# Zero products first, low parts by tile, outputs by column halves: another order at the two ends and the choice of a two-layer trunk

## The reference

```
x = x + concat(window_sink_attention(...), gated_retention(...)) @ w_out[l]    # from rms_norm(x) @ w_in[l], 2304 columns
h = rms_norm(x, ln_ffn[l])
y = swiglu(h, ...) if l == 0 else moe_swiglu(h, ...)       # D_FF = 2816
x = x + y
...
def moe_swiglu(h, router_w, w_gate, w_up, w_down):
    top_val, top_idx = lax.top_k(h @ router_w, 2)          # 2 of 8 experts for each token
    gates = sum over the two of one_hot(top_idx) * softmax(top_val)
    return sum over e of gates[..., e] * swiglu(h, w_gate[e], w_up[e], w_down[e])
...
return rms_norm(x, ln_final)
```

## Time and profile before

| | |
|---|---|
| median of 3 runs | 1190.61 us (1189.17 to 1190.63) |
| profiled execution: time, span | 1190.02 us, 1188.0 us |
| TensorE matmul, weight load busy | 1167.3 us (98%), 981.9 us (83%) |
| VectorE, ScalarE, GpSimd busy | 975.7 us (82%), 828.6 us (70%), 30.9 us (3%) |
| HBM read | 342.06 MB, 289 GB/s over the span |
| weight load to landing, experts | 7.0 us for 1 MB (median) |

### The profile page before, as it was taken

One profiled execution on the slowest core, in us unless ns is written; L12 is line 12 of the kernel. 1 busy time (PEld: TensorE's weight loads), 2 busy tenths in 40 slices (PEclk: granted clock), 3 DMA queues, 4 the chain that ended last, 5 costly groups with the idle time before them and its releaser, 6 DMA issues.

```text
span 1188.0 us, 18370 instructions
## 1 busy us (share of the span) xinstructions
PE 1167.3 (98%) x6010; PEld 981.9 (83%) x6010; DVE 975.7 (82%) x1101; ACT 828.6 (70%) x1007; POOL 30.9 (3%) x43
## 2 busy tenths in 40 slices
PE   7999999999999999999999999999999999999996
PEld 7997888888998788888888888888888888888885
DVE  4867555545675999999899999989999989999996
ACT  6655554534653788878778778868887877887884
POOL 0400000000120000000000000000000000000000
PEclk9999999999999999999999999999999999999999
DMA  9955655556444399999899999989999999999960
GB/s 284 370 182 164 196 192 194 177 183 207 142 161 142 109 376 364 395 342 368 330 338 369 372 373 360 355 331 347 362 396 342 361 336 338 375 365 368 366 238 35
DMA packets 142614, 344.64 MB, mean 290 GB/s; under 512 B 6112, under 2 KB 64688, under 8 KB 142528
## 3 DMA queue, kind: packets, MB, share of 16 engines
q1 hardware_dynamic: 141952, 342.34, 80.3%
q0 software_dynamic: 352, 1.09, 0.4%
q10 hardware_dynamic: 224, 0.10, 0.1%
HBM read 342.06 MB, written 1.44 MB: 289 GB/s over the span
## 4 chain that ended last, share of the span: by engine, by line
PE 91%; DVE 4%; ACT 2%; DMA 2%; issue 1%; SPq 0%; DVEq 0%; ACTq 0%
PE psum L1144 87%; PE psum L1141 4%; DMA raw<-in_w_in 1%; DVE prob L900 1%; DVE w_lo L381 0%; DVE smax L884 0%; DVE score L880 0%; ACT w_hi L372 0%; DMA skew<-bias_rows 0%; DVE nmax L885 0%; ACT aT_hi L590 0%; DVE x_sb L828 0%; ACT squares L578 0%; ACT aT_hi L726 0%; ACT w_hi L392 0%
## 5 line engine op out<-in xcount | busy, mean ns | idle before, releaser
L399 DVE TENSOR_TENSOR w_lo<-raw,w_hi 128x1024 fp32r<-128x1024 f32 x528 | 627.3, 1220 | 40.9 <-PE psum L1144 15.7
L392 ACT ACTIVATE w_hi<-raw 128x1024 fp32r<-128x1024 f32 x528 | 550.2, 1061 | 110.1 <-PE psum L1144 108.3
L1144 PE MATMUL psum<-w_hi,aT_hi 128*128 128x512 f32 (+1 forms) x1232 | 447.2, 372 | 1.4 <-ACT w_hi L372 0.6
L1144 PE MATMUL psum<-w_hi,aT_lo 128*128 128x512 f32 (+1 forms) x1232 | 440.0, 366 | 0.0
L1144 PE MATMUL psum<-w_lo,aT_hi 128*128 128x512 f32 (+1 forms) x1232 | 323.3, 366 | 0.8 <-DVE w_lo L381 0.7
L1144 PEld LDWEIGHTS psum<-w_hi,aT_hi 128*128 128x128 f32 x1232 | 233.4, 189 | 38.6 <-issue 1.8
L1144 PEld LDWEIGHTS psum<-w_hi,aT_lo 128*128 128x128 f32 x1232 | 233.6, 190 | 35.0
L1144 PEld LDWEIGHTS psum<-w_lo,aT_hi 128*128 128x128 f32 x1232 | 214.6, 189 | 40.4 <-DVE w_lo L399 1.8
L381 DVE TENSOR_TENSOR w_lo<-raw,w_hi 128x1024 fp32r<-128x1024 f32 x118 | 144.8, 1234 | 48.7 <-PE psum L1144 44.6
L372 ACT ACTIVATE w_hi<-raw 128x1024 fp32r<-128x1024 f32 x118 | 124.6, 1059 | 82.4 <-PE psum L1144 74.2
L1144 PE MATMUL psum<-w_hi,heT_hi 128*128 128x512 f32 x352 | 138.1, 392 | 0.0
(11 more groups left out here) (179 smaller groups left out, 638.5 us busy)
## 6 DMA issues: line engine op xcount, KB each, us to landing
raw<-in_exp_w_down SPq DMA_DIRECT2D x88, 1024.0 KB, 7.1
raw<-in_exp_w_gate SPq DMA_DIRECT2D x80, 1024.0 KB, 7.0
raw<-in_exp_w_up SPq DMA_DIRECT2D x80, 1024.0 KB, 6.9
raw<-in_w_in SPq DMA_DIRECT2D x17, 1024.0 KB, 5.4
raw<-in_ffn_w_gate SPq DMA_DIRECT2D x22, 512.0 KB, 4.0
raw<-in_ffn_w_up SPq DMA_DIRECT2D x22, 512.0 KB, 5.1
raw<-in_ffn_w_down SPq DMA_DIRECT2D x11, 1024.0 KB, 5.0
raw<-in_w_out SPq DMA_DIRECT2D x8, 1024.0 KB, 8.1
```

Source lines behind the costliest of these rows:

```text
L392: nc.scalar.activation(w_hi[:, q % HIGHS, :], raw_piece(slot, q % 2), ACT.Copy).then_inc(hi_made, 1)
L399: eng.tensor_tensor(w_lo[:, q % LOWS, :], raw_piece(e_slot[q // 2], q % 2), w_hi[:, q % HIGHS, :].bitcast(F32), ALU.subtract).then_inc(lo_ ...
L1144: return pe.matmul(dst, a, b, start=start, stop=stop, skip_group_check=True)
```

## The change

- **Start, TensorE.** VectorE clears two tiles of `aT_lo` first of all (its copy of the table rows moves behind the low part of piece 1). TensorE multiplies 8 products of zeros before it waits for anything loaded. The gain rows are turned before x. x's first half is turned, 6 more products of zeros follow, then piece 0, and only then x's second half. The bias products move from behind piece 0 to behind piece 1 and to other banks, and TensorE's wait for their copy moves from piece 2 to the turn of q and k.
- **Start, loads.** The first weight half is issued between the two halves of x; the second gain load moves from SP's queue to ScalarE's, ahead of the other one there.
- **Start, ScalarE.** The high part of piece 0 comes after two tiles of x, not four.
- **Choice.** `keep_busy` does 10 and 5 products instead of 8 and 3 behind the logits and the ranks. The gather goes by part and token tile, with a wait for one tile's low part at a time. ScalarE makes the high parts of pieces 0, 1 and 2 ahead of the loop (one of them ahead of the exponential) and has its table load there as well. VectorE splits the first two gathered banks and makes the low part of piece 0 ahead of the experts' weights and of the loop.
- **Experts.** Spreads and additions go by column halves: (half, tile) instead of (tile, half).
- **End.** The last two pieces go by column halves, so that the first half is announced (`down_half`) after six of the twelve products. ScalarE squares four half rows instead of two whole ones; one factor chain for both token tiles instead of two.

The diff, cut to its core:

```diff
-WARM_COPY, WARM_CHOICE, WARM_MARK = 2, 8, 3
+EARLY = 3
+WARM_COPY, WARM_CHOICE, WARM_MARK = 2, 10, 5
+START_BUSY, FIRST_BUSY = 8, 6
...
             load_x(0)
-            sp.dma_start(gain_rows[0:2 * DK, :], ln_mix.rearrange("l (k d) -> (l k) d", d=P)).then_inc(g_landed, 16)
+            load_first(0)
             load_x(1)
+            load_first(1)
...
             pool.wait_ge(gain_landed, 32)
-            pool.wait_ge(x_added, n * (4 * N_EXPERTS) + 10)
+            pool.wait_ge(x_added, n * (4 * N_EXPERTS) + 11)
...
             act.dma_start(cst[:, 0:P], consts[:, 0:P]).then_inc(i_landed, 16)
+            act.dma_start(gain_rows[0:2 * DK, :], ln_mix.rearrange("l (k d) -> (l k) d", d=P)).then_inc(g_landed, 16)
             act.dma_start(gain_rows[2 * DK:4 * DK, :], ln_ffn.rearrange("l (k d) -> (l k) d", d=P)).then_inc(g_landed, 16)
...
-                turned_high(n, range(4))
-                high(0 if layer == 0 else first - 1 + HIGHS)
+                if layer == 0:
+                    turned_high(n, range(2))
+                    high(0)
+                    turned_high(n, range(2, 4))
+                else:
+                    turned_high(n, range(4))
+                    high(first - 1 + HIGHS)
                 turned_high(n, range(4, DK))
...
             for t in range(TT):
                 act.wait_ge(xg_made, t + 1)
                 nc.scalar.activation(xg_hi[:, t, :], xg[:, t, :], ACT.Copy).then_inc(xg_hi_made, 1)
+            high_part_e(act, 0, 0)
             act.wait_ge(gap_made, 1)
             nc.scalar.activation(rc[4][:], rc[3][:], ACT.Exp).then_inc(e2_made, 1)
+            nc.scalar.activation(table_first[:], ssum[:, 0:1], ACT.Silu)
+            for q in range(1, EARLY):
+                high_part_e(act, 0, q)
...
+            def output_high(o, last=False, o_pass=0):
                 for b in range(2):
+                    if last and b == 0:
+                        act.wait_ge(down_half, o_pass + 1)
+                    else:
+                        act.wait_ge(piece_used, FFN_PIECES * o + (FRONT_PIECES + FFN_PIECES))
...
             with act.Fori(0, n_pass) as r:
-                nc.scalar.activation(table_first[:], ssum[:, 0:1], ACT.Silu)
+                with act.If(r > 0):
+                    for q in range(EARLY):
+                        high_part_e(act, N_EXPERTS * r, q)
...
+            for half in range(2):
+                for t in range(TT):
+                    cols = slice(512 * half, 512 * (half + 1))
+                    act.wait_ge(x_added, n_pass * (4 * N_EXPERTS) + (9 + 2 * half + t))
+                    nc.scalar.activation(squares[:, t, cols], x_sb[:, t, cols], ACT.Square,
+                                         accum_out=ssum_end[:, half, t:t + 1]).then_inc(squared, 1)
...
-            dve.wait_ge(t_landed, 32)
-            dve.tensor_copy(table_rows[:], table_sb[:].unsqueeze(2).to_broadcast([N_BUCKETS, ATT_HEADS, 64])).then_inc(rows_ready, 1)
+            dve.memset(aT_lo[:, DK - 2:DK, :].bitcast(F32), 0.0).then_inc(zeros_made, 1)
...
                 if layer == 0:
                     low(1)
+                    dve.wait_ge(t_landed, 32)
+                    dve.tensor_copy(table_rows[:], table_sb[:].unsqueeze(2).to_broadcast([N_BUCKETS, ATT_HEADS, 64])).then_inc(rows_ready, 1)
...
                 dve.tensor_tensor(xg_lo[:, t, :], xg[:, t, :], xg_hi[:, t, :].bitcast(F32), ALU.subtract).then_inc(xg_lo_made, 1)
+            for b in range(2):
+                gather_low(0, b)
+            low_part_e(dve, 0, 0)
             link.also(dve.tensor_scalar(posx[:, :, 8:16], posx[:, :, 0:8], -float(P), None, ALU.add))
...
             def vec_expert(r, e):
-                if e == 0:
-                    for b in range(2):
-                        gather_low(v, b)
-                for q in range(LOWS):
+                for q in range(1 if e == 0 else 0, LOWS):
                     low_part_e(dve, i, q)
...
+            def multiply_zeros(count):
+                for again in range(count):
+                    mm(bank(4), aT_lo[:, DK - 1, 0:P], aT_lo[:, DK - 2:DK, :].rearrange("p k t -> p (k t)"), True, True)
+            pe.wait_ge(zeros_made, 1)
+            multiply_zeros(START_BUSY)
             pe.wait_ge(i_landed, 16)
+            turn_h(0, (0,))
+            multiply_zeros(FIRST_BUSY)
...
                         piece(first + s, prods, tiles=tiles if u == 0 else None)
+                        if s == 0 and layer == 0:
+                            turn_h(0, (1,))
...
-                    if layer == 0 and s == 0:
+                    if layer == 0 and s == 1:
                         pe.wait_ge(rows_ready, 1)
...
-                for part in range(2):
+                for part, t in ((0, 0), (0, 1), (1, 0), (1, 1)):
+                    if part == 1:
+                        pe.wait_ge(xg_lo_made, t + 1)
                     for k in range(DK):
...
             def spread_out(o, v):
-                for t in range(TT):
-                    for half in range(2):
+                for half in range(2):
+                    for t in range(TT):
...
+            def last_two(i):
+                base = FFN_PIECES * i + FRONT_PIECES
+                for half in range(2):
+                    cols = slice(512 * half, 512 * (half + 1))
+                    for q in (FFN_PIECES - 2, FFN_PIECES - 1):
+                        mm(bank(6 + half), heT_hi[:, q - GU_PIECES, :], w_hi[:, q % HIGHS, cols], False, False)
+                        mm(bank(6 + half), heT_lo[:, q - GU_PIECES, :], w_hi[:, q % HIGHS, cols], False, False)
+                    for q in (FFN_PIECES - 2, FFN_PIECES - 1):
+                        ins = mm(bank(6 + half), heT_hi[:, q - GU_PIECES, :], w_lo[:, q % LOWS, cols], False, q == FFN_PIECES - 1)
...
```

More of the change, by code:

```diff
@@ L156, in trunk @@
         ssum = sb("ssum", [P, 2])
+        ssum_end = sb("ssum_end", [P, 2, 2])
         rvar = sb("rvar", [P, 8])
@@ L1144, in mm, with turn_h @@
                 return pe.matmul(dst, a, b, start=start, stop=stop, skip_group_check=True)
-            def turn_h(n):
-                for half in range(2):
+            def turn_h(n, halves=range(2)):
+                for half in halves:
+                    if n == 0 and half == 0:
+                        pe.wait_ge(g_landed, 32)
+                        pe.matmul(psum[:, 7, 2 * REL:2 * REL + 4 * DK], gain_rows[:], ident[0:4 * DK, 0:4 * DK], is_transpose=True,
+                                  start=True, stop=True, skip_group_check=True).then_inc(gain_turned, 1)
                     if n == 0:
```

90 lines of the change are left out of this document (48 added, 42 removed).

## The result

The changed kernel takes 1198.45 us (median of 4 runs, 1198.12 to 1198.77) against 1189.91 us before (1189.17 to 1190.63): 1.0070 times as long, 95% interval 1.0054 to 1.0086. Slower, as forecast, but by 8.5 us where 3.2 were forecast, and above the range's 1196.8. (The forecast started from 1190.61, the median before of that time, which is 0.7 us higher.) The profiled execution took 1198.12, its span is 1196.1, 8.1 more than before.

A forecast was written before the change was run, and what follows sets the result against it. TensorE, busy 98%, was taken to bound the kernel, though not the chain of the first 40 us. Start +2.9, choice +0.9 and end -0.6 sum to +3.2, giving 1193.8 us, range 1189.0 to 1196.8.

The forecast's parts named there:

- the loop entry: Choice: reading the number of passes and entering the loop, no longer hidden, adds 0.64 us; bounds 0.2 and 1.7.
- The zero products: Start: eight zero products run from 1.3 to 4.7, ahead of x at 5.0, and cost nothing.
- The gain loads: Start: second gain load, issued at 1.70 instead of 1.22, takes 3.7 us, so 5.4 to 5.6; 0.5 later.
- The second half of x behind piece 0: Start: x's second half is turned after the whole first piece, by 14.2; the bias copy ends 3.2 late.
- I take the clock as full from the first piece on: Start: TensorE runs at full clock from piece 0 on; if piece 0 runs at 1.2 GHz, +2.0 us more.
- The loads behind the copy: Start: loads of skew, constants and unit 5 behind the bias copy meet an emptier queue, giving 0.3 us back.
- a TensorE wait for it of 1 to 2 us: Choice, a sign of being right: TensorE waits 1 to 2 us for w_lo of piece 1.
- The sum of the half squares: End: after the last half square, one sum, the variance and the root take 0.7 us together.
- Faster: Rival, start: first weights land by some 5.3, bias copy not late, full clock pays; -4.3, 1186.3 us; chance 0.14.
- Costs less: Rival, start, choice and end: weights and gains early, loop entry at lower bound; +1.2, 1191.8 us; chance 0.22.
- The clock is not raised: Rival, start and choice: piece 0 at 1.2 GHz, gather as before; +6.7, 1197.3 us; chance 0.06.
- the clock falls: Rival, start: clock falls in the new stand before piece 1, +1.7 more; +4.9, 1195.5 us; chance 0.18.

The follow-up runs named there:

- gains_back: Changed kernel with the mixer's gain rows back on SP's queue behind x's first half; 1196.85 us, 1.0063.
- x_second_first: Changed kernel with the second half of x turned ahead of piece 0 again; 1195.16 us, 1.0046.
- choice_filled: Changed kernel with eight more products on an idle bank in TensorE's wait for w_lo of piece 1 of expert 0; 1198.72 us, 1.0081.
- weights_first: Changed kernel with the expert weights computed ahead of the gathered low parts and the first w_lo; 1195.39 us, 1.0053.
- three_low: Changed kernel with w_lo of pieces 0 to 2, not of piece 0 alone, ahead of the expert weights; 1198.1 us, 1.0077.
- best1: Start of the kernel before, choice of weights_first, last pieces by column halves, spreads, additions, squares and factors by token tile; 1188.36 us, 0.9986.
- end_only: Kernel before with the change's end alone, including spreads and additions by column halves; 1190.12 us, 1.0005.
- zeros_only: Kernel before with only the cleared tiles and eight zero products ahead of everything; 1188.64 us, 0.9994.
- start_back: Changed kernel with the whole start of the kernel before, keeping the change's choice and end; 1192.66 us, 1.0021.
- stand_filled: Changed kernel with ten more products on an unused bank in the stand before piece 1; 1198.2 us, 1.0071.
- gains_x_back: Changed kernel with the mixer's gain rows back on SP's queue and x's second half turned ahead of piece 0; 1193.38 us, 1.0032.
- best2: best1 with the eight zero products of zeros_only; 1188.21 us, 0.9988.

## Why the prediction was right in direction and wrong in size

Most mechanisms of the sum were there. What failed is the overlap and the clock: the sum took TensorE's clock as full behind every new stand, priced the late gain load and the loop entry too low, and took one small sum at the end as short. The span's 8.1 is 5.2 + 3.0 + 0.2 - 0.35 and 0.03. Above the forecast's 3.2 lie 4.9: 1.5 and 1.4 for two falls of the clock, 1.2 for the late tile 4 (0.7 of it the gain rows), 0.6 for the loop entry, 0.8 for the end, and small terms of either sign, which take back 0.6.

**Start, +2.9 forecast, +5.2 measured.** *The zero products* ran from 1.47 to 5.25 (forecast 1.3 to 4.7); the memset took 0.5. *The gain loads* are the first step that failed: "5.4 to 5.6" was 7.52, since I moved the later issue (1.70 instead of 1.22) into the sum with the duration of the earlier one. In the trace of before the load in that very place of ScalarE's queue, the bucket table of 24 KB issued at 1.70, took 4.6 us, which would have given 6.3: nearer, though still short. That gains_back turned x at 5.56 shows the place as the cause; which of the large loads held it up is not separated. The first weights had landed at 6.89 and waited for TensorE, so their forecast of 8.5 was not tested.

*The second half of x behind piece 0* was the right mechanism: x_second_first gives 3.45, of which 2.9 are tile 4 and 1.26 the stand and fall before piece 1, less 0.7 behind the copy. Tile 4 came at 15.41 instead of 14.2, 0.7 of that from the gain rows.

*"I take the clock as full from the first piece on"* is the second step that failed, twice. Behind the stand before piece 1, forecast at 2.6 us and 2.38 long, the clock fell. That was a rival, with 0.18 and 1.7 us; the traces show 1.67 to 1.68 us of waiting at the bias copy where it fell and 0.18 where it held, so it cost 1.5. Its chance was too small: behind this stand of 2.38 us it fell in three profiled executions (the changed kernel, gains_back, choice_filled) and held in two (weights_first, three_low). The kept gap of 1.50 us was no guide to it. And ahead of piece 0 the zero products did not do what they were there for: behind the 2.40 us for the gain rows the changed kernel's clock was down again until 12 us, and in the five other executions with these late gain rows x's first half was turned at half the pace, and the first zero products behind it still took 0.43 us each. The turns of the changed kernel, and of choice_filled:

```profile
7.80 1.27 PE L1174 MATMUL psum<-cst,x_sb 128*128 128x128 f32 x8
```
```profile
8.08 1.97 PE L1174 MATMUL psum<-cst,x_sb 128*128 128x128 f32 x8
```

*The loads behind the copy* gave back 0.94 (15.71 us from the copy's end to the turn, 16.65 before), not 0.3. In sum 1.2 + 1.8 - 0.65 above the forecast.

**Choice, +0.9 forecast, +3.0 measured.** The gather at full clock: right, and the first gathered low part came 0.92 earlier by the gather's start (forecast 1.03). The expert weights on VectorE's path: 1.23, as forecast. *The loop entry*: 1.25 instead of 0.64, inside its bounds of 0.2 to 1.7; I had taken ScalarE's 0.92 for VectorE. The prediction took the entry as hidden only by a wait; weights_first shows that long operations of VectorE's own hide it too, the way to lose neither term. So w_lo of piece 1 is 1.56 late, and this alone makes 26.03 + 1.56 = 27.6, the choice of every profiled execution with this order in which the clock held. The missing term, the third step that failed, is the wait's own effect: I forecast "a TensorE wait for it of 1 to 2 us" among the signs and gave it no price. It was 1.98, the clock fell behind it, and that costs 1.43 (29.02 against 27.59 in choice_filled). I had weighed such a fall only for the stand before piece 1, and put it at nothing here without a reason.

**End, -0.6 forecast, +0.2 measured.** The additions ended 1.08 earlier (forecast 0.98). Then two things. The sum of the half squares was counted with the variance and the root at 0.7 in all, and took 0.90 alone: it starts beside GpSimd's product, and it ends at 1188.93, when that ends (1186.57 + 2.35 = 1188.92). And ScalarE's first output now needs the factor of both tiles, which is ready at 7.8 us behind the last product, where the forecast had 7.16; by tile, in best1, the output was issued at 8.13. The forecast compared the factors' common end with the second one of before, and that was sound; it failed by the 0.7 of the sum.

**The experts** were forecast at nothing and took 0.35 less. end_only has the same (761.61), and best1, with spreads and additions by tile, took 761.92. That points at their new order, which holds for every expert, and not at the start or the choice. It is not shown: zeros_only, with the old order, took 761.79, between the two. How it comes about I did not follow.

**The rivals.** "Faster" asked for the first weights by 5.3; in the changed kernel they landed at 6.9, and where ScalarE waited for them, at 8.0 and 8.9. "Costs less" needed early gain rows and a cheap loop entry, and had neither. "The clock is not raised" is refuted for most of piece 0 (products of 0.12 us from 12.04 on) and for the gather, not for the turns of x's first half. Two stands with a falling clock, of which one was a rival with a chance of 0.18 and one had none, make 2.9 of the 4.9 us by which the forecast of the sum missed. That the time came out slower was forecast for the right reason; but with the sum of the rival "the clock falls", +4.9, it would still have been 3.2 short.

**What stays open.** Whether the clock falls behind a given wait differs between executions: behind 1.98 us at the choice it fell in the changed kernel, start_back and stand_filled, and held in gains_back, gains_x_back and x_second_first; before the turn of q and k it held behind 2.03, 2.19 and 2.37 us (the changed kernel, weights_first, choice_filled) and fell behind 2.23, 2.51, 2.58, 2.60 and 2.73 (gains_back, three_low, stand_filled, gains_x_back, x_second_first), at 1.5 to 1.6 us each. A wait of 1.63 us was followed by a fall in best2 (ahead of piece 0) and by none in three_low (at the choice). Longer stands fell more often, but the length alone does not decide. In the three falls at the choice the clock went down 1.04 to 1.05 us behind the end of the wait; what decides between the executions, no run here shows.

## What to carry to other kernels

A stand of TensorE costs its length and, in some executions, the clock behind it: where a change makes one of 2 us on the path, put a price on the fall (here 1.4 to 1.6 us each) even where the nearest gap in the old trace kept full clock. Small operations that filled a wait of their engine are free only there; before moving them, look what the engine does next, and sum its work up to the piece that it sets. Entering a loop cost 1.25 us behind small operations that wait for one another and nothing behind long ones. And a load that is waited for is costed by where it stands, not by its size: the same 8 KB took 3.7 us in one place and 5.8 in the next. Price it from the load that held that place in the old trace.

## What the runs showed of the hardware

- VectorE's operations with two operands in SBUF stood still while GpSimd ran its product. ssum, 0.90 us beside it, ended with it to 0.01 us; in best1 the first product of the factor took 0.48 us (1178.72 to 1179.20, with GpSimd's end at 1179.18) and the next ones of the same size 0.16. One-input operations (0.15 to 0.17) and additions with one operand in PSUM (0.74 with and without it) were not touched. The Trainium skill ("GPSIMD Engine Reference", "1. Specifications") says that VectorE instructions with two SBUF inputs contend with GpSimd; the traces agree.
- Behind one and the same wait, of 1.98 us at the choice and of 2.38 us before piece 1, the clock fell in some profiled executions and held in others. One profile of a kernel does not size such a wait.
- Reading a register from memory and entering a loop took VectorE 1.50 us from the start of the read to the first operation in the loop (410.94 to 412.44) where nothing covered it, and left no gap where operations of 0.7 to 1.2 us were still being worked off (weights_first, read at 407.42).
- The granted clock reads 1.00 in the first microseconds of before, while products of 256 columns come every 0.213 us, the 1.2 GHz spacing.
